# Hybrid decoder layer on one core: feed-forward activations turned by VectorE and DMA, compressed-branch products split

## What is computed

```
def _swiglu(x, w_gate, w_up, w_down):
    return (jax.nn.silu(x @ w_gate) * (x @ w_up)) @ w_down      # hidden width 5632

h = x
h = _layer_norm(A * h + 0.5 * _swiglu(h, ffn1 weights), ...)
mix = _mixer(h, ...)          # two attention branches, 22 column chunks of projections, merge, w_o
h = _layer_norm(A * h + mix, ...)
h = _layer_norm(A * h + 0.5 * _swiglu(h, ffn2 weights), ...)
```

## Time and profile before

| | |
|---|---|
| median of the runs | 2210.73 us |
| the profiled execution's own time | 2210.37 us |
| its span in the profile | 2208.6 us |
| granted TensorE clock, mean | 0.999 of full speed |
| TensorE busy (matmul) | 2195.1 us, 99% |
| VectorE, ScalarE busy | 1235.2 us (56%), 957.5 us (43%) |
| DMA, mean over the span | 192 GB/s |

### The profile page before, as it was taken

The page is one execution under the profiler, slowest core; times in us unless marked ns, Lnnn a source line. Parts: engine busy times, 40 slices in busy tenths (PEclk is TensorE's granted clock), DMA queues, the critical chain, the costliest instruction groups (busy, mean ns, idle before and its releaser), DMA issues.

```text
span 2208.6 us, 26996 instructions
## 1 busy us (share of the span) xinstructions
PE 2195.1 (99%) x10028; PEld 1816.8 (82%) x10028; DVE 1235.2 (56%) x1224; ACT 957.5 (43%) x1119; POOL 7.7 (0%) x12
## 2 busy tenths in 40 slices
PE   9999999999999999999999999999999999999998
PEld 8888888888888888888788888888888888888886
DVE  5555545554454767776655647566455555544445
ACT  5444444443333644544354444364434444443332
POOL 0000000000000000000000000000000000000000
PEclk9999999999999999999999999999999999999999
DMA  8556556666656666656567576656665565566664
GB/s 298 185 186 202 179 188 190 199 219 199 192 193 196 179 194 194 212 168 169 155 179 203 164 223 194 201 163 200 191 190 185 188 194 190 179 235 194 193 193 141
DMA packets 220459, 424.94 MB, mean 192 GB/s; under 512 B 16352, under 2 KB 17120, under 8 KB 219360
## 3 DMA queue, kind: packets, MB, share of 16 engines
q1 hardware_dynamic: 220096, 423.38, 61.8%
q10 hardware_dynamic: 288, 0.52, 0.1%
HBM read 420.18 MB, written 3.68 MB: 192 GB/s over the span
## 4 chain that ended last, share of the span: by engine, by line
PE 98%; DVE 1%; ACT 0%; DMA 0%; issue 0%; DVEq 0%; ACTq 0%
PE acc L522 31%; PE acc L523 30%; PE acc L528 30%; PE bank L561 1%; PE bank L1864 1%; PE acc L1611 1%; PE acc L1618 1%; PE acc L1614 1%; PE bank L1706 0%; PE bank L1813 0%; PE bank L1835 0%; PE bank L1917 0%; PE bank L1914 0%; PE bank L1817 0%; DVE w_lo L512 0%; PE bank L1853 0%
## 5 line engine op out<-in xcount | busy, mean ns | idle before, releaser
L512 DVE TENSOR_TENSOR w_lo<-raw,w_hi 128x1024 fp32r<-128x1024 f32 x768 | 928.5, 1224 | 570.2 <-ACT w_hi L505 563.2
L505 ACT ACTIVATE w_hi<-raw 128x1024 fp32r<-128x1024 f32 x766 | 802.4, 1058 | 831.1 <-PE acc L528 760.5
L522 PE MATMUL acc<-w_hi,act_hi 128*128 128x512 f32 x2160 | 853.1, 395 | 0.0
L523 PE MATMUL acc<-w_hi,act_lo 128*128 128x512 f32 x2160 | 841.8, 390 | 0.0
L528 PE MATMUL acc<-w_lo,act_hi 128*128 128x512 f32 x2160 | 579.6, 389 | 0.0
L522 PEld LDWEIGHTS acc<-w_hi,act_hi 128*128 128x128 f32 x2160 | 405.8, 188 | 85.8 <-issue 3.2
L528 PEld LDWEIGHTS acc<-w_lo,act_hi 128*128 128x128 f32 x2160 | 405.3, 188 | 86.0 <-DVE w_lo L512 0.9
L523 PEld LDWEIGHTS acc<-w_hi,act_lo 128*128 128x128 f32 x2160 | 405.9, 188 | 81.2
L522 PE MATMUL acc<-w_hi,hT_hi 128*128 128x512 f32 x688 | 267.9, 389 | 0.0
L523 PE MATMUL acc<-w_hi,hT_lo 128*128 128x512 f32 x688 | 267.7, 389 | 0.0
L528 PE MATMUL acc<-w_lo,hT_hi 128*128 128x512 f32 x688 | 185.2, 389 | 0.0
(11 more groups left out here) (236 smaller groups left out, 863.6 us busy)
## 6 DMA issues: line engine op xcount, KB each, us to landing
raw<-in_ffn_w_down_dram SPq DMA_DIRECT2D x176, 512.0 KB, 4.5
raw<-in_w_in_dram SPq DMA_DIRECT2D x176, 512.0 KB, 4.0
raw<-in_ffn_w_gate_dram SPq DMA_DIRECT2D x175, 512.0 KB, 4.4
raw<-in_ffn_w_up_dram SPq DMA_DIRECT2D x175, 512.0 KB, 4.4
raw<-in_w_o_dram SPq DMA_DIRECT2D x32, 512.0 KB, 4.8
raw<-in_cmp_kv_w_dram SPq DMA_DIRECT2D x16, 512.0 KB, 4.1
raw<-in_w_branch_a_dram SPq DMA_DIRECT2D x16, 512.0 KB, 5.1
raw<-in_w_branch_b_dram SPq DMA_DIRECT2D x8, 512.0 KB, 4.8
```

Source lines behind the costliest of these rows:

```text
L505: nc.scalar.activation(weights(n0, s if isinstance(i, int) and i == 0 else s + per)[0], raw[:, r, :], ACT.Copy).then_inc(hi_done, 1)
L512: nc.vector.tensor_tensor(lo, raw[:, r, :], hi.bitcast(F32), ALU.subtract).then_inc(lo_done, 1)
L522: nc.tensor.matmul(o, a_hi[:, kt0 + k, at], hi, start=first and k == 0, stop=False)
L523: nc.tensor.matmul(o, a_lo[:, kt0 + k, at], hi, start=False, stop=False)
```

## The change

It leaves the slots and their order as they are.

Feed-forward: TensorE's `h_task` is gone. VectorE forms the product in place in `gate_t`, then, at its step s=2, turns it in 32x32 blocks (`turn_blocks`, one instruction on 128x1024). SP issues 16 DMAs for each chunk, two after each of the loads n = 7 to 14; each moves 32 partitions with 8 runs of 32 elements (128 B), from `hid` to `hT_lo`. At s=15 ScalarE rounds `hT_lo` into `hT_hi` in one instruction of 128x1024, and VectorE subtracts in place. For the last chunk the same happens at slots 7 to 15 of the down product. SP's loop over the down slots is written out.

Compressed branch: the stationary operand of `cmp_out`'s value products has 124 columns in place of 60, with the second copy from column 64; ScalarE writes `vcmp_hi`, VectorE `vcmp_lo` (four instructions, at position 98); the transposed probabilities are kept as hi and lo parts in `pT_cmp`; `values` makes two float32r matmuls of 512 columns in place of one float32. `kvcmp` is placed at CMP_END + 16 and not + 11. The exponentials of unit 0 come one position later, and `rope_sum` moves from step 1 to step 2.

```diff
-        for i in range(GU_CHUNKS):
-            for half in range(2):
-                task(("h", f, i, half), half)
...
-    place(("kvcmp",), CMP_END + 11)
+    place(("kvcmp",), CMP_END + 16)
...
+            def place_h(f, i, n):
+
+                if n == PLACE_FROM:
+                    sp.wait_ge(h_turned, i + GU_CHUNKS * f)
+                for v in range(2 * (n - PLACE_FROM), 2 * (n - PLACE_FROM) + 2):
+                    b, q = divmod(v, QUADS)
+                    src = hid_kt[QUAD * b:QUAD * b + QUAD].rearrange("p k t (q j) -> p (k t) q j", q=QUADS)[:, :, q, :]
+                    dst = h_chunk(hT_lo[QUAD * q:QUAD * q + QUAD], i).bitcast(F32)
+                    dst = dst.rearrange("p k t (b j) -> p (k t) b j", t=TILES, b=QUADS)[:, :, b, :]
+                    sp.dma_start(dst, src).then_inc(h_placed[f], 16)
...
+                    if not isinstance(i, int) and PLACE_FROM <= n < PLACE_FROM + 8:
+                        place_h(f, i, n)
...
+            def round_h(f, i):
+
+                act.wait_ge(h_placed[f], i * (16 * QUADS * QUADS))
+                nc.scalar.activation(h_chunk(hT_hi, i), h_chunk(hT_lo, i).bitcast(F32), ACT.Copy).then_inc(h_rounded, 1)
...
+                exp_at[pl.at[("s", u, 0 if kind == CMP else n_blocks(u) - 1)] + LAG + (2 if u == 0 else 1)] = u
...
+                nc.vector.tensor_tensor(gate_t[:, :, :], gate_t[:, :, :], acc_pair(1), ALU.mult).then_inc(acc_emptied[1], 1)
+
+            def turn_blocks(f, i):
+
+                dve.wait_ge(acc_emptied[1], i + (gu_acc[f] // 2))
+                nc.vector.transpose(hid_kt.rearrange("p k t n -> p t k n"), gate_t[:, :, :].rearrange("p t (k n) -> p t k n", n=P)) \
+                    .then_inc(h_turned, 1)
+
+            def split_h(f, i):
+
+                dve.wait_ge(h_rounded, i + GU_CHUNKS * f)
+                lo = h_chunk(hT_lo, i)
+                nc.vector.tensor_tensor(lo, lo.bitcast(F32), h_chunk(hT_hi, i).bitcast(F32), ALU.subtract).then_inc(h_split, 1)
...
+                else:
                     dve.wait_ge(emptied, c // 2 + 1)
                     rope_sum(dst[:, :, 0:w], heads)
...
-                        if not peel and h == 0 and s == 3:
-                            for half in range(2):
-                                h_task(f, i, half)
...
+                        if c == 0 and s in (0, DOWN_SLOTS - 4, DOWN_SLOTS - 2):
+                            pe.wait_ge(h_split, GU_CHUNKS * f + (GU_CHUNKS if s == DOWN_SLOTS - 2 else GU_CHUNKS - 1 if s else GU_CHUNKS - 2))
...
-                    nc.tensor.matmul(bank[:, t.bank, :], pT[0:HPG * N_CMP, tile, 0, :],
-                                     vcmp[:, g].rearrange("p h n -> p (h n)"), start=True, stop=True).then_inc(bank_filled, 1)
+                    for v, (vals, n) in enumerate(((vcmp_hi, KV_ROWS), (vcmp_lo, HPG * N_CMP))):
+                        mm = nc.tensor.matmul(bank[:, t.bank, :], pT_cmp[0:n, tile, :], vals[0:n, g].rearrange("p h n -> p (h n)"),
+                                              start=v == 0, stop=v == 1)
+                    mm.then_inc(bank_filled, 1)
```

More of the change, by code:

```diff
@@ L53 @@
 SPARE = 2
+QUAD = 32
+QUADS = P // QUAD
+PLACE_FROM = 7
+H_ROUND = 15
 ALPHA = 2.0 ** 0.25
@@ L294, in build @@
         over = ExitStack()
+        hid4 = sb("hid4", [P, 2, GROUPS, KV_ROWS], F32, over)
+        over.close()
+        over = ExitStack()
         cmp_sum = sb("cmp_sum", [KV_ROWS, CMP_HIDDEN], F32, over)
@@ L310, in build @@
         hid = sb("hid", [P, TILES, COLS], F32, over)
+        over.close()
+        over = ExitStack()
+        vcmp_hi = sb("vcmp_hi", [P, GROUPS, HPG, HEAD], F32R, over)
+        sb("bufs_1_2", [P, 2, TILES, COLS], F32, over)
+        vcmp_lo = sb("vcmp_lo", [P, GROUPS, HPG, HEAD], F32R, over)
         over.close()
@@ L333, in build @@
         s1 = sb("s1", [P, HPG, TOKENS])
+        over = ExitStack()
+        pT_cmp = sb("pT_cmp", [P, TILES, P], F32R, over)
+        over.close()
         pT = sb("pT", [P, 3, HPG, P])
@@ L401, in build @@
         gate_tanh = sem("gate_tanh")
+        h_turned = sem("h_turned")
+        h_placed = [sem("h_placed0"), sem("h_placed1")]
+        h_rounded = sem("h_rounded")
+        h_split = sem("h_split")
         var_ready = sem("var_ready")
@@ L419, in build @@
         gelu_out = sem("gelu_out")
+        vcmp_rounded = sem("vcmp_rounded")
         folds_ready = sem("folds_ready")
@@ L744, in ffn @@
                     load_ln(2)
[L745 to L749, removed]
+                for c in range(OUT_CHUNKS):
+                    for s in range(DOWN_SLOTS):
+                        load_slot(sp, rows(w_dn[f])[:, 2 * s:2 * s + 2, c * COLS:(c + 1) * COLS], down_slot[f], 0, 0,
+                                  c * DOWN_SLOTS + s)
+                        if c == 0 and PLACE_FROM <= s < PLACE_FROM + 8:
+                            place_h(f, GU_CHUNKS, s)
             def load_ln(which):
@@ L1042, in gu_chunk @@
                         up_half(f, i)
-                    if not peel and s in (5, 6):
-                        split_h(f, i, s - 5)
+                    if not peel and s == 2:
+                        turn_blocks(f, i)
+                    if not peel and s == H_ROUND:
+                        split_h(f, i)
                     if s == (GATE_END if peel and f == 0 else GU_SLOTS - 1) + LAG:
@@ L1456, in _ @@
                                                         gelu_x[:, 0], ALU.add, ALU.mult))
[L1457 to L1460, removed]
-                    ins.then_inc(gelu_out, 1)
+                    link(nc.vector.memset(hid4[:, :, :, HPG * N_CMP:V_ROW], 0.0))
+                    for g in range(GROUPS):
+                        one = hidT[:, :, 1, g * N_CMP:(g + 1) * N_CMP].unsqueeze(2).broadcast_to([P, 2, HPG, N_CMP])
+                        for at in (0, V_ROW):
+                            ins = nc.vector.tensor_copy(hid4[:, :, g, at:at + HPG * N_CMP].rearrange("p k (h n) -> p k h n", h=HPG),
+                                                        one)
+                    ins.then_inc(gelu_out, 1)
+                if pos == max(pl.at[("kvcmp",)], pl.at[("qT", UNITS.index((CMP, 0, 0)), 1)]) + LAG + 1:
+                    t, n = T[("kvcmp",)], HPG * N_CMP
+                    dve.wait_ge(vcmp_rounded, 1)
+                    wait_filled(dve, T[("qT", UNITS.index((CMP, 0, 0)), 1)])
+                    for h in range(HPG):
+                        ins = nc.vector.scalar_tensor_tensor(vcmp_lo[0:n, :, h, :], values_in_bank(t, n), own_head[0:n, h:h + 1],
+                                                             vcmp_hi[0:n, :, h, :].bitcast(F32), ALU.mult, ALU.subtract)
+                    ins.then_inc(bank_emptied[t.bank], 1)
                 for step in range(3):
```

75 lines of the change are left out of this document (27 added, 48 removed).

## The result

The changed kernel takes 2188.78 us (2186.9 to 2189.12, four runs) against 2210.81 us: a ratio of 0.990, 95% interval 0.9888 to 0.9911, 22.0 us less. Its profiled execution took 2186.9 us, span 2185.1, which is 23.5 us under the profiled one of before. The forecast was 2187.0, in a range of 2184 to 2196. All executions of both kernels showed the same granted clock, 0.998 to 0.999.

The account below looks back on a forecast made before the run. PE's unbroken matmul stream was taken as the bound, so removed width shortens the kernel. Transposes 19.6, compressed branch 3.2 and shifts 1.0 sum to 23.8 us, giving 2186.6 from 2210.37, adjusted to 2187.0; range 2184 to 2196.

Parts of the forecast that it names:

- Transposes, 19.6 us: Feed-forwards: removing eight transposes from PE's stream saves 0.89 us in each of 22 chunks; 17.6 us at the low end.
- VectorE, nothing on the path: Feed-forward chunks: the block transpose takes 1.22 us on VectorE and delays splits without making PE wait.
- The cover: Slot 3's split, behind VectorE's block transpose, ends 4.9 us before PE wants it; over 2 with a 4.0 us transpose.
- SP: Sixteen more DMAs a chunk at 0.6 us issue each stay off the path; 11 us of lateness are spare.
- DMA engines: Placing 128 B pieces at 12.7 ns adds 3.3 us of engine time a chunk, hidden; share about 0.67.
- The point of decision, 66 ns: Time per 128 B placing piece at which DMA engine time would fill a chunk's 43.5 us.
- The wait at s=15: ACT's wait for placed blocks is met: they land at T + 27 to 30, ACT arrives at T + 33.7.
- Compressed branch, 3.2 us: Mixer: two float32r matmuls (0.45 us) replace one float32 product (1.25), saving 0.80 four times; 2.4 us if less.
- The shifts, 1.0 us: Mixer: exponentials and rope_sum one position later remove PE waits, 1.0 us taken between 0 and 1.9.
- The slow one: Rival: DMA engines become the bound; about 2380 us at 104 ns a piece, chance 0.06.
- The mild one: Rival: late blocks make PE wait at the next chunk's start, 0.35 us a chunk, 2195 us; chance 0.06.
- The third: Rival: PE's slot pace is set by something that fills the removed time; chance within the 0.04.

Follow-up runs that it names:

- a1: The changed kernel run again unaltered, beside the kernel before (2210.44 us): 2187.13 us, ratio 0.9894.
- e1: The kernel before with only the feed-forward part of the change, all mixer edits left out: 2190.35 us.
- e7: The changed kernel with eight unused 128x128 transposes put back on TensorE after slot 3 in 20 chunks: 2205.32 us.
- e4_turn_x4: The changed kernel with VectorE's block transpose done four times over, each waiting for the last: 2187.6 us.
- e5: The changed kernel with four more small DMAs (32 partitions, 64 B each) from SP in each of slots 7 to 14: 2392.57 us.
- e2: The kernel before with the feed-forward part and the two one-position shifts (exponentials of unit 0, rope_sum), without the compressed branch's products: 2189.15 us.
- e3: The changed kernel with the compressed branch's second product (vcmp_lo) on 124 rows in place of 60: 2186.05 us.
- e6: The changed kernel with one more SBUF-to-SBUF DMA of 128 B pieces in each of 16 slots of chunks 1 to 10: 2519.48 us.
- e8: The changed kernel with ScalarE's wait for the placed blocks at step 12 in place of 15: 2187.29 us.
- e9: The changed kernel with ScalarE's wait for the placed blocks at step 10 in place of 15: 2230.15 us.
- e4_turn_x8: The changed kernel with VectorE's block transpose done eight times over, each waiting for the last: 2317.61 us.

## Why the prediction was right, point by point

**The bound.** Right: PE's stream kept its 2.72 us pace and the width of what was taken out came off the end.

**The sum, 23.8 us.** Measured 23.3 (a1); 22.0 in the first result. That it came so near is in part luck: by the runs the transposes brought 0.5 more than forecast, the compressed branch 1.2 less and the shifts 0.2 more, and these offset each other.

**Transposes, 19.6 us.** Measured 20.1 (e1), 10.2 and 10.0 in the two feed-forwards of the profile (9.8 and 10.0 in a1's); putting 20 of 22 back costs 17.7 to 18.2 (e7). Reading starts instead of the 22.8 us of busy time was what mattered.

**VectorE, nothing on the path.** Right, at 1.24 us for the transpose against 1.22 taken. The cover held four of them (e4_turn_x4), not eight.

**SP.** Right that it hides, off in two sizes: a small DMA is 0.61 us long and 0.69 with what lies between, and the room is not 11 us but 7.6, since it has to be regained in each chunk (e5).

**DMA engines.** Right that 128-byte pieces stay cheap: 12.7 ns taken, 12.9 measured for one packet. The share still rose to 0.71 and not 0.67: 0.71 x 43.5 - 0.59 x 44.4 = 4.7 us a chunk in place of 3.3, or 18 ns a piece with all that comes along. What came along and was left out of the sum is that the 256 weight pieces grew from 104 to 109 ns, 1.4 us a chunk. The point of decision, 66 ns, was far away. Of the two passages of the Trainium skill that the prediction set against each other, that of VectorE: DVE Perf Modes (The three transpose paths) puts its factor of 19 on copies whose innermost stride at the destination is large. The copies here write runs of 128 B, so they lie outside that condition, which the prediction didn't give, and nothing here tests the factor. That of DMA: Bandwidth & Descriptors (Why small descriptors are slow), that transfers within SBUF don't suffer the penalty of small pieces, agrees with the trace only in part: 12.9 ns for 128 B are 0.10 ns a byte, 104 ns for 2048 B are 0.05, so a byte in small pieces took twice as long.

**The wait at s=15.** Met, with 3.5 us to spare. The step that put the end of the last pair's issue at T + 23.2 was wrong: it ended at T + 27.3 (336.19 + 1.37, with T = 310.26, two slots ahead of 315.70), and the blocks landed at T + 30.4, just outside the T + 27 to 30 of the prediction. I had left out that VectorE, at its step 9, stands waiting for the gate's tanh, with split 10 behind it (timeline of DVE):

```profile
333.28 1.22 DVE L1083 SCALAR_TENSOR_TENSOR gate_t<-gate_t,acc 128x1024 f32<-128x1024 f32 x1 [4.18 <-ACT gate_t L872]
```

So load 14 and the pair behind that are late. The landing, 3.7 us, was just under the near end of 4 to 7 and gave some of it back.

**Compressed branch, 3.2 us.** The term that was mis-sized: 2.0 in the runs (e2 to a1), 4 x 0.41 = 1.6 in the timeline. The pair was priced as two full matmuls; the one on 60 rows was longer itself, and so were the steps before and behind it, 0.84 us in place of 0.47 (e3).

**The shifts, 1.0 us.** Measured 1.2 (e1 to e2), and the waits at the compression slots went with them.

**Rivals.** The slow one needs 66 ns a piece, and e6 shows 12.9 to 14.6. The mild one needs blocks that land 11 us later than they do; e8 and e9 bear out sums of this kind. The third, that removed time is filled by something else, falls with e1, where the time went down by the transposes' width, and with e7, where it came back.

## What to carry to other kernels

Where one engine's stream has no gaps, price an edit by the starts around it, and ask of the work that moves only how late it may be. That room has two bounds: how far ahead the queue is, and how much of it comes back before the next burst; the smaller counts. Mind the row count of a short matmul in such a stream: here one on 60 rows cost 0.37 us more than the same padded to 124 (e3), half of it in the steps beside it.

## What the runs showed of the hardware that I had not expected

A matmul of 512 columns on 60 rows held the stream for 0.42 us, the one on 124 rows ahead of it for 0.32 and the 128-row one behind it for 0.33, where each takes 0.23 to 0.24 once all have 124 or 128 rows (changed kernel and e3).

Small DMAs from SP took it some 0.6 us each whether they moved 256 pieces of 128 B (placing, 612 ns) or 32 pieces of 64 B (e5, four in 2.51 us).

A packet of 128 B from SBUF to SBUF took 12.9 ns of a DMA engine, and the more of them there were, the longer the 2 KB weight packets took: 104 ns on average before, 109 in the changed kernel, 119 in e6.

In e4_turn_x8 stalls of about 4 us in each chunk brought the granted clock to 0.50 for the next 5 us, and that cost 44 us on top of the 86 us of the stalls; in e5, where TensorE waited 92 times for 1.5 us on average, the mean clock was 0.982; in e9 one stall of some 2 us a chunk left it at 0.997.
